# A fused decoder block on one core: the operand sums of the first feed-forward chunk split over several slots, and the chunk loops written out

## The chip, the cores and the metric

The kernel runs on one NeuronCore of a Trainium2 chip. The metric is the device time of one launch in microseconds (us), the median over several runs.

## What is computed

One decoder layer on 256 tokens of width 2048, in float32: a SwiGLU feed-forward (FFN1), a mixer (short gated convolution beside sparse attention), a second SwiGLU (FFN2), and a last RMSNorm.

```python
def rmsnorm(x, g):
    xf = x.astype(jnp.float32)
    y = xf * lax.rsqrt(jnp.mean(xf * xf, axis=-1, keepdims=True) + EPS)
    return (y * g.astype(jnp.float32)).astype(x.dtype)

def swiglu(h, wg, wu, wd):
    return (jax.nn.silu(h @ wg) * (h @ wu)) @ wd

    x = x + 0.5 * swiglu(rmsnorm(x, ffn1_norm[i]), ffn1_wg[i], ffn1_wu[i], ffn1_wd[i])
    x = x + hybrid_mixer(rmsnorm(x, mix_norm[i]), w_in[i], ...)
    x = x + 0.5 * swiglu(rmsnorm(x, ffn2_norm[i]), ffn2_wg[i], ffn2_wu[i], ffn2_wd[i])
return rmsnorm(x, final_norm)
```

Only the gate and up parts of the two feed-forwards matter here: (256 x 2048) times (2048 x 5632), twice.

## The kernel before

**Numbers.** Each float32 product is made from three matmuls. An operand is split into a high part (rounded, on ScalarE) and a low part (the rest, on VectorE), and `hi*hi + hi*lo + lo*hi` is summed in PSUM. The transposed activations are `hT_hi` and `hT_lo` (16 tiles of 128 rows), a weight block is `w_hi` and `w_lo`.

**Slots.** The whole kernel is a row of slots. A slot is one weight block of 2 x 128 rows by 512 columns (512 KB). SyncE loads it into one of four buffers `raw`, and waits for that until VectorE has finished the block that lay there (`lo_ready`). ScalarE makes `w_hi` (L1307), VectorE `w_lo` (L1825), TensorE multiplies it by both token tiles: 12 matmuls of 512 columns (L768 to L770, function `group`). Every engine has its own instruction queue, written in slot order with other work put between slots by hand-made tables (`after`), and the engines meet only in semaphores.

**Pairs (seven products).** Some neighbouring slots (kinds `PAIR`, `PAIR2`) are done by a Strassen-like scheme with 7 block products for 8 (`seven_products`, L786 to L788). It needs sums of the four 128 x 128 activation blocks of a "quad" (two k tiles by two token tiles), called `hs`, and sums of weight blocks, called `wt` (VectorE `weight_sums`, L1887 to L1892, and `wt_low`, L1897; ScalarE L1358). Three quads of a feed-forward have activation sums; quad number 0 belongs to k tiles 2 and 3, numbers 1 and 2 to tiles 4 to 7. `hs` holds four blocks a quad, split again into `hs_hi` (ScalarE, `hs_high`, L1389) and `hs_lo` (VectorE, `hs_low`, L1934). The function `h_sums` makes `hs`: one addition of `hT_hi` and `hT_lo` (L1921), two sums that need only that (L1925, L1926), then a third (L1928) that needs the first, and a fourth (L1930) that needs the third.

**Chunks.** The 5632 columns are 11 chunks of 512, 16 slots each. Chunk 0 has the table `FIRST`, the others `CHUNK` or, for chunks 5, 6 and 10, `CHUNK3`. Quads 1 and 2 are used in every chunk (the pairs of `FIRST` stand in slots 8, 9 and 12, 13), quad 0 in `CHUNK3` alone:

```python
FIRST = [(GATE, 0), (GATE, 1), (UP, 0), (UP, 1), (GATE, 4), (GATE, 5), (UP, 4), (UP, 5),
         (PAIR, 2), (PAIR2, 2), (GATE, 6), (GATE, 7), (PAIR, 3), (PAIR2, 3), (UP, 6), (UP, 7)]
THREE = (5, 6, 10)
LATE = (0,) + THREE
H_QUAD = {1: 0, 2: 1, 3: 2}
```

In chunk 0 of FFN1 the activations are still being brought in. TensorE transposes x four k tiles at a time between slots (L835), ScalarE and VectorE make `hT_hi` (L1330) and `hT_lo` (L1853) of them ("operand n"), ScalarE also squares x for the norm (`sq`, L1343), and VectorE makes the variance (L1866, L1870). What stands behind which slot of chunk 0 of FFN1 on VectorE:

```python
after = {2: [op[1]], 3: [lambda: h_sums(0)], 4: [op[2]], 5: [lambda: hs_low(0)],
         6: [op[3], lambda: variance(RS_FFN1, DM, NDC)],
         7: [lambda: inverse_root(RS_FFN1)]}
```

**From chunk 0 to chunk 1.** Chunk 0 is `LATE`: its products are only gathered in the first slots of chunk 1. ScalarE copies product 1 to `z` when the second pair is done (L1385), VectorE adds it to the gate's bank (L1956, `gate_products`), ScalarE applies silu to the first token tile (a table load, then L1399), makes `w_hi` of slot 1, and applies silu to the second tile. TensorE may begin chunk 1 only after both silus (`silu_done`), since it writes the same banks. `h_sum` shares its memory with `z`.

**Loops.** On TensorE, ScalarE and VectorE chunks 2, 3, 4 and chunks 8, 9 of each feed-forward are turns of a hardware loop (`Fori`), in which waits compare with registers. The other chunks are written out. GpSimd moves the gated product `gu` with DMAs in a loop of its own. Between chunk 5 and 6, and at the end, stand the down projections (`down`).

**In chunk n** VectorE also makes the sums `gs` of chunk n - 1's gated product (`gu_sums`, L2037 to L2042) and the low parts (`gu_operand`: L2050 for `guT_lo`, L2055 for `gs_lo`); `quad_no` says whether the chunk has such sums: it has for chunks 0 to 3 and 6 to 8.

## Time and profile before

| | us |
|---|---|
| median of 3 runs (lowest 1814.9, highest 1815.92) | 1815.18 |
| the profiled execution | 1815.7 |
| its span, from the first to the last instruction | 1813.9 |
| TensorE matmuls busy | 1802.4 |
| VectorE busy | 1534.1 |
| ScalarE busy | 1017.5 |
| GpSimd busy | 247.0 |

The profiled execution took 0.5 us more than the median, and 1.8 us of it lie outside the span. Busy times are of one engine each and overlap. A matmul is listed with a modelled length (0.39 us for 512 columns) that is longer than the time from one start to the next (0.227 us), since matmuls are pipelined: gaps of TensorE are therefore read from start to start. The granted clock of TensorE is 0.999 over the span.

### The profile page before, as it was taken

The numbers are of one execution on the slowest core, as the hardware profiler recorded it, in microseconds if no ns is written. First come the engines' busy times: TensorE is split into PE (matmuls) and PEld (weight loads), VectorE is DVE, ScalarE is ACT, GpSimd is POOL, SyncE is SP. The second block draws the span as 40 slices with busy tenths as digits, with TensorE's granted clock in tenths as the row PEclk, the third lists the DMA queues.
The fourth block names the chain that finished last, engine by engine and source line by source line (L and its number), as shares of the span: only waits on it lengthen the run. The fifth ranks groups of instructions, "written<-read, shape, count | busy, mean of one in ns | idle before, by whom it ended". The sixth has DMA issues, their size and how long they took to land.

```text
span 1813.9 us, 22660 instructions
## 1 busy us (share of the span) xinstructions
PE 1802.4 (99%) x8151; PEld 1485.4 (82%) x8152; DVE 1534.1 (85%) x1821; ACT 1017.5 (56%) x1320; POOL 247.0 (14%) x442
## 2 busy tenths in 40 slices
PE   9999999999999999999999999999999999999998
PEld 6888888888888888888788888888888888888886
DVE  7998898889999987678667867899898889988987
ACT  7555555445555556556577745555555455555554
POOL 2111111001111100000123300111111000221100
PEclk9999999999999999999999999999999999999999
DMA  7777766667676666766543655667766666777764
GB/s 244 220 211 212 217 206 211 206 200 218 211 211 207 215 199 210 209 212 195 150 137 108 209 175 185 215 211 214 213 205 207 215 204 195 216 213 217 246 200 150
DMA packets 199277, 367.13 MB, mean 202 GB/s; under 512 B 19012, under 2 KB 23856, under 8 KB 199056
## 3 DMA queue, kind: packets, MB, share of 16 engines
q1 hardware_dynamic: 185008, 352.37, 63.2%
q0 software_dynamic: 11648, 12.02, 2.2%
q10 hardware_dynamic: 2528, 1.52, 0.3%
q8 instruction: 56, 0.92, 0.2%
q14 instruction: 37, 0.30, 0.1%
...
## 4 chain that ended last, share of the span: by engine, by line
PE 97%; DVE 1%; ACT 1%; DMA 0%; issue 0%; SPq 0%; ACTq 0%; DVEq 0%
PE ps L768 25%; PE ps L770 24%; PE ps L769 24%; PE ps L786 7%; PE ps L787 7%; PE ps L788 7%; PE ps L835 1%; DMA raw<-in_ffn_wu_dram 0%; DVE w_lo L1825 0%; PE ps L1071 0%; PE ps L1098 0%; PE ps L1073 0%; PE ps L1099 0%; PE ps L1201 0%; ACT w_hi L1307 0%
## 5 line engine op out<-in xcount | busy, mean ns | idle before, releaser
L1825 DVE TENSOR_TENSOR w_lo<-raw,w_hi 128x1024 fp32r<-128x1024 f32 x579 | 702.1, 1227 | 132.6 <-ACT w_hi L1307 127.9
L1307 ACT ACTIVATE w_hi<-raw 128x1024 fp32r<-128x1024 f32 x579 | 609.4, 1058 | 357.4 <-PE ps L770 271.5
L768 PE MATMUL ps<-w_hi,hT_hi 128*128 128x512 f32 x1356 | 531.1, 392 | 1.2 <-DVE hT_lo L1853 1.1
L770 PE MATMUL ps<-w_hi,hT_lo 128*128 128x512 f32 x1356 | 528.3, 390 | 0.0
L769 PE MATMUL ps<-w_lo,hT_hi 128*128 128x512 f32 x1356 | 528.0, 389 | 0.0
L709 POOL DMA_DIRECT2D gu_raw<-gu_sq x352 | 187.1, 540 | 1077.3 <-DVE gu_sq L2061 1003.0
L768 PEld LDWEIGHTS ps<-w_hi,hT_hi 128*128 128x128 f32 x1356 | 254.7, 188 | 53.7 <-DVE hT_lo L1853 1.5
L770 PEld LDWEIGHTS ps<-w_hi,hT_lo 128*128 128x128 f32 x1356 | 254.5, 188 | 53.8
L769 PEld LDWEIGHTS ps<-w_lo,hT_hi 128*128 128x128 f32 x1356 | 254.7, 188 | 51.5
L1358 ACT ACTIVATE wt_hi<-wt 128x1024 fp32r<-128x1024 f32 x152 | 160.2, 1054 | 230.2 <-DVE wt L1887 230.2
L768 PE MATMUL ps<-w_hi,guT_hi 128*128 128x512 f32 x496 | 193.1, 389 | 0.0
L770 PE MATMUL ps<-w_hi,guT_lo 128*128 128x512 f32 x496 | 193.0, 389 | 0.0
L769 PE MATMUL ps<-w_lo,guT_hi 128*128 128x512 f32 x496 | 193.0, 389 | 0.0
L1897 DVE TENSOR_TENSOR wt_lo<-wt,wt_hi 128x1024 fp32r<-128x1024 f32 x152 | 185.3, 1219 | 0.0
L770 PEld LDWEIGHTS ps<-w_hi,guT_lo 128*128 128x128 f32 x496 | 93.1, 188 | 19.4
L768 PEld LDWEIGHTS ps<-w_hi,guT_hi 128*128 128x128 f32 x496 | 93.1, 188 | 19.3
L769 PEld LDWEIGHTS ps<-w_lo,guT_hi 128*128 128x128 f32 x496 | 93.1, 188 | 19.2
L1887 DVE TENSOR_TENSOR wt<-raw 128x1024 f32<-128x1024 f32 x76 | 93.0, 1224 | 15.1 <-PE ps L788 10.5
L731 POOL TENSOR_SCALAR prob<-prob,sums,gate 128x128 f32<-128x128 f32 (+1 forms) x64 | 37.2, 590 | 258.8 <-DVE sums L2323 258.8
L786 PE MATMUL ps<-wt_hi,hs_hi 128*128 128x512 f32 x150 | 58.6, 391 | 0.8 <-DVE wt_lo L1897 0.7
L788 PE MATMUL ps<-wt_hi,hs_lo 128*128 128x512 f32 x150 | 58.4, 389 | 0.0
L787 PE MATMUL ps<-wt_lo,hs_hi 128*128 128x512 f32 x150 | 58.4, 389 | 0.0
...
## 6 DMA issues: line engine op xcount, KB each, us to landing
...
```

Source lines behind the costliest of these rows:

```text
L709: pool.dma_start(gu_raw[c_ * SQ:c_ * SQ + SQ, :, a_, :], gu_sq[a_ * SQ:a_ * SQ + SQ, :, c_ * P:c_ * P + P]).then_inc(gu_moved, 16)
L768: mm(o, x_hi, w_hi[:, s, kk, :], start=begin, stop=False, skip_group_check=skip)
L769: mm(o, x_hi, w_lo[:, s, kk, :], start=False, stop=False, skip_group_check=skip)
L770: ins = mm(o, x_lo, w_hi[:, s, kk, :], start=False, stop=last and kk == GK - 1, skip_group_check=skip)
L786: mm(o, x_hi, y_hi, start=start, stop=False, skip_group_check=True)
L787: mm(o, x_hi, y_lo, start=False, stop=False, skip_group_check=True)
L788: return mm(o, x_lo, y_hi, start=False, stop=stop, skip_group_check=True)
L1307: act.activation(w_hi[:, c % SLOTS, :, :], raw[:, c % SLOTS, :, :], ACT.Copy).then_inc(hi_ready, 1)
L1358: act.activation(wt_hi[:, 2 * half:2 * half + 2, :], wt[:, 2 * half:2 * half + 2, :], ACT.Copy).then_inc(t_hi_ready, 1)
L1825: tt(w_lo[:, s, :, :], raw[:, s, :, :], w_hi[:, s, :, :].bitcast(F32), ALU.subtract).then_inc(lo_ready, 1)
L1887: tt(wt[:, T1:T3 + 1, :], w[:, 2, :].unsqueeze(1).to_broadcast([P, 2, CH]), w[:, 0::3, :], ALU.subtract).then_inc(t1_ready, 1)
L1897: tt(wt_lo[:, sl, :], wt[:, sl, :], wt_hi[:, sl, :].bitcast(F32), ALU.subtract).then_inc(t_lo_ready, 1)
```

## The change

Three things are done.

1. The activation sums of chunk 0 are made in pieces, in both feed-forwards. `h_sums(f, late, step)` works on quads 1 and 2 (`late` 0) or on quad 0 (`late` 1), and its step 1 is the third and fourth sum. On VectorE in FFN1 step 0 for two quads stays behind slot 3, step 1 stands behind slot 5, and `hs_low` for two quads behind slot 6. In FFN2 both steps stay behind slot 2. Quad 0 follows behind slot 14 in both, its `hs_low` behind slot 8 of chunk 1. On ScalarE `hs_high` for two quads moves in FFN1 from behind slot 4 to behind slot 5, ahead of the squares of x; for quad 0 it stands behind slot 15. TensorE waits for two quads before the first pair of chunk 0, and for quad 0 before the first pair of chunk 5 (`THREE[0]`).
2. The subtraction that makes `gs_lo` is taken out of `gu_operand` into `gs_low`, which stands behind slot 14 in `CHUNK3` chunks and behind the same slot as before in the others.
3. The hardware loops over chunks on TensorE, ScalarE and VectorE are replaced by written-out chunks. GpSimd's loop stays.

```diff
@@ TensorE @@
                     if p == chunk_pairs(0)[0]:
-                        pe.wait_ge(hs_lo_ready, f + 1)
+                        pe.wait_ge(hs_lo_ready, 2 * f + 1)
...
                     for p, (kind, q) in enumerate(chunk_table(n)):
+                        if n == THREE[0] and p == at_[0]:
+                            pe.wait_ge(hs_lo_ready, 2 * f + 2)
...
-                chunk(1)
-                with pe.Fori(0, QUADS[0] - 1) as i:
-                    chunk(2, i)
-                for n in range(QUADS[0] + 1, PARTN[0]):
+                for n in range(1, PARTN[0]):
                     chunk(n)
                 down(0)
-                chunk(PART0[1])
-                chunk(PART0[1] + 1)
-                with pe.Fori(0, QUADS[1] - 1) as i:
-                    chunk(PART0[1] + 2, i)
-                for n in range(PART0[1] + QUADS[1] + 1, NFC):
+                for n in range(PART0[1], NFC):
                     chunk(n)
                 down(1)
@@ ScalarE @@
-            def hs_high(f):
-                act.wait_ge(hs_ready, f + 1)
-                act.activation(hs_hi[:, :, :, :], hs[:, :, :, :], ACT.Copy).then_inc(hs_hi_ready, 1)
+            def hs_high(f, late):
+
+                sl = slice(0, 1) if late else slice(1, 3)
+                act.wait_ge(hs_ready, 2 * f + late + 1)
+                act.activation(hs_hi[:, sl, :, :], hs[:, sl, :, :], ACT.Copy).then_inc(hs_hi_ready, 1)
...
-                    after = {1: [sq[0]], 2: [op[1]], 3: [sq[1]], 4: [op[2], lambda: hs_high(0)],
-                             5: [sq[2]], 6: [op[3], sq[3]], 7: [lambda: root(RS_FFN1)], 10: [vectors]}
+                    after = {1: [sq[0]], 2: [op[1]], 3: [sq[1]], 4: [op[2]],
+                             5: [lambda: hs_high(0, 0), sq[2]], 6: [op[3], sq[3]], 7: [lambda: root(RS_FFN1)], 10: [vectors], 15: [lambda: hs_high(0, 1)]}
                 else:
-                    after = {2: [lambda: x_square(RS_FFN2, NDC - 1, resid(R_ATT, NDC - 1))], 3: [lambda: hs_high(1)],
-                             5: [lambda: x_operand(2, NDC - 1)], 6: [lambda: root(RS_FFN2)]}
+                    after = {2: [lambda: x_square(RS_FFN2, NDC - 1, resid(R_ATT, NDC - 1))], 3: [lambda: hs_high(1, 0)],
+                             5: [lambda: x_operand(2, NDC - 1)], 6: [lambda: root(RS_FFN2)], 15: [lambda: hs_high(1, 1)]}
@@ VectorE @@
+            def h_sums(f, late, step):
+
+
+                sl = slice(0, 1) if late else slice(1, 3)
+                no, k0, quads = 2 * f + late + 1, 2 if late else 4, 1 if late else 2
+                h = h_sum[:, sl, :].rearrange("p q (r t) -> p q r t", r=2)
                 block_ = lambda t, kk: h[:, :, kk, t * P:t * P + P]
...
+                o = lambda n: hs[:, sl, n - 1, :]
+                if step == 0:
+                    for b in range(2):
+                        dve.wait_ge(free[4 + b], operand_use(2 if f else 0, b, 1) + 1)
+                    pick = lambda buf: buf[:, k0:k0 + 2 * quads, :].rearrange("p (q r) t -> p q r t", q=quads)
+                    tt(h, pick(hT_hi).bitcast(F32), pick(hT_lo).bitcast(F32), ALU.add).then_inc(hs_full, 1)
+                    dve.wait_ge(hs_full, no)
+                    tt(o(1), block_(1, 0), block_(1, 1), ALU.add).then_inc(hs1_ready, 1)
+                    tt(o(3), block_(1, 0), block_(0, 0), ALU.subtract)
+                else:
+                    dve.wait_ge(hs1_ready, no)
+                    tt(o(2), o(1), block_(0, 0), ALU.subtract).then_inc(hs2_ready, 1)
+                    dve.wait_ge(hs2_ready, no)
+                    tt(o(4), block_(0, 1), o(2), ALU.subtract).then_inc(hs_ready, 1)
...
-                if quad is not None:
-                    dve.wait_ge(gs_hi_ready, count(quad + 1, i, 1))
-                    low, buf, high = gs_parts(n, i)
-                    ins = tt(low, buf, high.bitcast(F32), ALU.subtract)
-                ins.then_inc(gu_lo, 1)
+                if quad is None:
+                    ins.then_inc(gu_lo, 1)
+
+            def gs_low(n, quad, i=None):
+
+                if quad is not None:
+                    dve.wait_ge(gs_hi_ready, count(quad + 1, i, 1))
+                    low, buf, high = gs_parts(n, i)
+                    tt(low, buf, high.bitcast(F32), ALU.subtract).then_inc(gu_lo, 1)
...
-                    after = {2: [op[1]], 3: [lambda: h_sums(0)], 4: [op[2]], 5: [lambda: hs_low(0)],
-                             6: [op[3], lambda: variance(RS_FFN1, DM, NDC)],
+                    after = {2: [op[1]], 3: [lambda: h_sums(0, 0, 0)], 4: [op[2]], 5: [lambda: h_sums(0, 0, 1)],
+                             6: [op[3], lambda: hs_low(0, 0), lambda: variance(RS_FFN1, DM, NDC)],
                              7: [lambda: inverse_root(RS_FFN1)]}
...
+                after[14] = [lambda: h_sums(f, 1, 0), lambda: h_sums(f, 1, 1)]
...
+                            if n == 1 and p == 8:
+                                hs_low(f, 1)
...
+                            if p == (14 if n in THREE else gu_at + 1):
+                                gs_low(n - 1, quad_no(f, n - 1), i)
```

(ScalarE's and VectorE's loops are replaced as TensorE's.) The line numbers in the changed kernel differ from those before: on VectorE the `h_sum` addition is L1916, the four sums L1918, L1919, L1922, L1924, `hs_lo` L1930, `w_lo` L1815 and operands L1843; on ScalarE `w_hi` is L1302, `hs_hi` L1386, operands L1325 and squares L1338.

VectorE in FFN1, chunk 0, from slot 3 to slot 6, before. A bracket names the semaphores that an instruction waits for.

```order
L1825 TENSOR_TENSOR w_lo<-raw,w_hi 128x1024 [waits hi_ready]
L1921 TENSOR_TENSOR h_sum<-hT_hi,hT_lo 128x1536 [waits bank_free5,bank_free4]
L1925 TENSOR_TENSOR hs<-h_sum 128x3x128 [waits hs_full]
L1926 TENSOR_TENSOR hs<-h_sum 128x3x128
L1928 TENSOR_TENSOR hs<-hs,h_sum 128x3x128 [waits hs1_ready]
L1930 TENSOR_TENSOR hs<-h_sum,hs 128x3x128 [waits hs2_ready]
L1825 TENSOR_TENSOR w_lo<-raw,w_hi 128x1024 [waits hi_ready]
```

The same place now; the four rows of operand 2 stand between:

```order
L1815 TENSOR_TENSOR w_lo<-raw,w_hi 128x1024 [waits hi_ready]
L1916 TENSOR_TENSOR h_sum<-hT_hi,hT_lo 128x1024 [waits bank_free5,bank_free4]
L1918 TENSOR_TENSOR hs<-h_sum 128x2x128 [waits hs_full]
L1919 TENSOR_TENSOR hs<-h_sum 128x2x128
L1815 TENSOR_TENSOR w_lo<-raw,w_hi 128x1024 [waits hi_ready]
L1843 SCALAR_TENSOR_TENSOR hT_lo<-ps,vecs,hT_hi 128x256 [waits operand_hi]
L1843 SCALAR_TENSOR_TENSOR hT_lo<-ps,vecs,hT_hi 128x256
L1843 SCALAR_TENSOR_TENSOR hT_lo<-ps,vecs,hT_hi 128x256 [waits operand_hi]
L1843 SCALAR_TENSOR_TENSOR hT_lo<-ps,vecs,hT_hi 128x256
L1815 TENSOR_TENSOR w_lo<-raw,w_hi 128x1024 [waits hi_ready]
L1922 TENSOR_TENSOR hs<-hs,h_sum 128x2x128 [waits hs1_ready]
L1924 TENSOR_TENSOR hs<-h_sum,hs 128x2x128 [waits hs2_ready]
```

The third and fourth sum, which `hs_high` waits for, moved behind the `w_lo` of slot 5, and all sums are two quads wide, not three.

ScalarE in the same stretch, from operand 2's last instructions to the `w_hi` of slot 6, before:

```order
L1330 ACTIVATE hT_hi<-ps,vecs 128x256
L1389 ACTIVATE hs_hi<-hs 128x1536 [waits hs_ready]
L1307 ACTIVATE w_hi<-raw 128x1024 [waits group_done,landed1]
L1343 ACTIVATE junk,ssq<-x 128x512 [waits x_landed2]
L1343 ACTIVATE junk,ssq<-x 128x512 [waits act_step]
L1307 ACTIVATE w_hi<-raw 128x1024 [waits act_step,group_done,landed2]
```

Now:

```order
L1325 ACTIVATE hT_hi<-ps,vecs 128x256
L1302 ACTIVATE w_hi<-raw 128x1024 [waits group_done,landed1]
L1386 ACTIVATE hs_hi<-hs 128x1024 [waits hs_ready]
L1338 ACTIVATE junk,ssq<-x 128x512 [waits x_landed2]
L1338 ACTIVATE junk,ssq<-x 128x512 [waits act_step]
L1302 ACTIVATE w_hi<-raw 128x1024 [waits act_step,group_done,landed2]
```

`hs_hi` and the `w_hi` of slot 5 changed places; the squares and the `w_hi` of slot 6 stay behind both.

VectorE from the end of the second pair of chunk 0 to the gate's addition (the same in both feed-forwards), now; before, the five rows from `h_sum` to the last `hs` were not there:

```order
L1887 TENSOR_TENSOR wt_lo<-wt,wt_hi 128x1024 [waits t_hi_ready]
L1815 TENSOR_TENSOR w_lo<-raw,w_hi 128x1024 [waits hi_ready]
L1916 TENSOR_TENSOR h_sum<-hT_hi,hT_lo 128x512 [waits bank_free5,bank_free4]
L1918 TENSOR_TENSOR hs<-h_sum 128x128 [waits hs_full]
L1919 TENSOR_TENSOR hs<-h_sum 128x128
L1922 TENSOR_TENSOR hs<-hs,h_sum 128x128 [waits hs1_ready]
L1924 TENSOR_TENSOR hs<-h_sum,hs 128x128 [waits hs2_ready]
L1815 TENSOR_TENSOR w_lo<-raw,w_hi 128x1024 [waits hi_ready] x2
L1952 TENSOR_TENSOR ps<-ps,z 128x512 [waits prod1_copied]
```

Five instructions stand new between slot 14's `w_lo` and the two `w_lo` of slot 15 and of chunk 1's slot 0.

## Rows read from the trace of the kernel before

**Rows 1.** First part of the page: busy time, share, instructions

```profile
PE 1802.4 (99%) x8151; PEld 1485.4 (82%) x8152; DVE 1534.1 (85%) x1821; ACT 1017.5 (56%) x1320; POOL 247.0 (14%) x442
```

**Rows 2.** Timeline, PE, chunk 0 of FFN1: start us, us, instruction [idle before <-releaser]

```profile
20.77 0.39 PE L770 MATMUL ps<-w_hi,hT_lo 128*128 128x512 f32 x1
22.25 0.50 PE L768 MATMUL ps<-w_hi,hT_hi 128*128 128x512 f32 x1 [1.09 <-DVE hT_lo L1853]
...
36.61 0.50 PE L786 MATMUL ps<-wt_hi,hs_hi 128*128 128x512 f32 x1 [0.73 <-DVE wt_lo L1897]
...
37.67 0.50 PE L786 MATMUL ps<-wt_hi,hs_hi 128*128 128x512 f32 x1
```

**Rows 3.** Windows, chunk 2 of FFN1: us, busy (x) PE PEld DVE ACT POOL, clock

```profile
99.68:143.20 43.52, 43.52 (x193) 36.04 (x192) 38.98 (x46) 22.81 (x25) 8.50 (x16) 1.00 0.75 224
```

**Rows 4.** Timeline, DVE, slots 3 to 5 of chunk 0 of FFN1

```profile
16.40 1.75 DVE L1921 TENSOR_TENSOR h_sum<-hT_hi,hT_lo 128x1536 f32<-128x1536 f32 x1
...
18.66 0.55 DVE L1926 TENSOR_TENSOR hs<-h_sum 128x384 f32<-128x384 f32 x1
19.13 0.55 DVE L1928 TENSOR_TENSOR hs<-hs,h_sum 128x384 f32<-128x384 f32 x1
19.72 0.56 DVE L1930 TENSOR_TENSOR hs<-h_sum,hs 128x384 f32<-128x384 f32 x1
20.20 1.22 DVE L1825 TENSOR_TENSOR w_lo<-raw,w_hi 128x1024 fp32r<-128x1024 f32 x1
21.33 1.65 DVE L1853 SCALAR_TENSOR_TENSOR hT_lo<-ps,vecs,hT_hi 128x256 fp32r<-128x256 f32 x4
```

**Rows 5.** Timeline, ACT, slots 4 to 10 of chunk 0 of FFN1

```profile
18.03 1.57 ACT L1330 ACTIVATE hT_hi<-ps,vecs 128x256 fp32r<-128x256 f32 x4 [0.50 <-PE ps L835]
...
21.70 1.04 ACT L1307 ACTIVATE w_hi<-raw 128x1024 fp32r<-128x1024 f32 x1
22.65 0.61 ACT L1343 ACTIVATE junk<-x 128x512 bf16<-128x512 f32 x1
...
24.28 1.06 ACT L1307 ACTIVATE w_hi<-raw 128x1024 fp32r<-128x1024 f32 x1 [0.17 <-ACT junk L1343]
...
28.90 1.06 ACT L1307 ACTIVATE w_hi<-raw 128x1024 fp32r<-128x1024 f32 x1 [0.17 <-ACT junk L1343]
...
37.38 0.23 ACT L1299 ACTIVATE vecs<-ps 128x104 f32<-128x104 f32 x1
```

**Rows 6.** Timeline, DVE, slots 7 and 8 of chunk 0 of FFN1

```profile
30.00 1.30 DVE L1825 TENSOR_TENSOR w_lo<-raw,w_hi 128x1024 fp32r<-128x1024 f32 x1 [0.56 <-ACT w_hi L1307]
...
31.41 1.23 DVE L1825 TENSOR_TENSOR w_lo<-raw,w_hi 128x1024 fp32r<-128x1024 f32 x1
32.56 1.41 DVE L1887 TENSOR_TENSOR wt<-raw 128x1024 f32<-128x1024 f32 x1
```

**Rows 7.** Timeline, DVE, ACT and PE where FFN1's chunk 1 begins

```profile
47.26 3.49 DVE L1825 TENSOR_TENSOR w_lo<-raw,w_hi 128x1024 fp32r<-128x1024 f32 x3
51.55 0.70 DVE L1956 TENSOR_TENSOR ps<-ps,z 128x512 f32<-128x512 f32 x1 [0.80 <-ACT z L1385]
...
55.16 0.68 ACT L1399 ACTIVATE gu<-ps,rs 128x512 f32<-128x512 f32 x1
...
56.16 0.39 PE L768 MATMUL ps<-w_hi,hT_hi 128*128 128x512 f32 x1
```

**Rows 8.** Timeline, DVE, the same place in FFN2

```profile
1146.66 3.61 DVE L1825 TENSOR_TENSOR w_lo<-raw,w_hi 128x1024 fp32r<-128x1024 f32 x3
1151.92 0.70 DVE L1956 TENSOR_TENSOR ps<-ps,z 128x512 f32<-128x512 f32 x1 [1.65 <-ACT z L1385]
```

**Rows 9.** Timeline, DVE, 128-wide sums in chunk 1 of FFN1

```profile
84.80 0.29 DVE L2037 TENSOR_TENSOR gs<-gu_raw 128x128 f32<-128x128 f32 x1
...
85.20 0.29 DVE L2040 TENSOR_TENSOR gs<-gs,gu_raw 128x128 f32<-128x128 f32 x1
85.53 0.29 DVE L2042 TENSOR_TENSOR gs<-gu_raw,gs 128x128 f32<-128x128 f32 x1
```

More of the change, by code:

```diff
@@ L1491, in down @@
                                 x_operand(1, 0)
-                chunk(1)
-                with act.Fori(0, QUADS[0] - 1) as i:
-                    chunk(2, i)
-                for n in range(QUADS[0] + 1, PARTN[0]):
+                for n in range(1, PARTN[0]):
                     chunk(n)
                 down(0)
-                chunk(PART0[1])
-                chunk(PART0[1] + 1)
-                with act.Fori(0, QUADS[1] - 1) as i:
-                    chunk(PART0[1] + 2, i)
-                for n in range(PART0[1] + QUADS[1] + 1, NFC):
+                for n in range(PART0[1], NFC):
                     chunk(n)
@@ L1935, in hs_low @@
+            def hs_low(f, late):
+                sl = slice(0, 1) if late else slice(1, 3)
+                dve.wait_ge(hs_hi_ready, 2 * f + late + 1)
+                tt(hs_lo[:, sl, :, :], hs[:, sl, :, :], hs_hi[:, sl, :, :].bitcast(F32),
                    ALU.subtract).then_inc(hs_lo_ready, 1)
@@ L2161, in down @@
                                 final_gains((23, 25, 39).index(g))
-                chunk(1)
-                with dve.Fori(0, QUADS[0] - 1) as i:
-                    chunk(2, i)
-                for n in range(QUADS[0] + 1, PARTN[0]):
+                for n in range(1, PARTN[0]):
                     chunk(n)
                 down(0)
-                chunk(PART0[1])
-                chunk(PART0[1] + 1)
-                with dve.Fori(0, QUADS[1] - 1) as i:
-                    chunk(PART0[1] + 2, i)
-                for n in range(PART0[1] + QUADS[1] + 1, NFC):
+                for n in range(PART0[1], NFC):
                     chunk(n)
```

22 lines of the change are left out of this document (3 added, 19 removed).

## The prediction

> **What bounds the kernel now.** I read the page first: TensorE's matmuls are busy 1802.4 us of a span of 1813.9 [rows 1], so only what shortens or lengthens TensorE's waits can change the time. Then I looked for every place where two matmuls start further apart than usual. In a chunk the usual distance is 43.52 us / 192 = 0.227 us [rows 3]. In the timeline of TensorE three waits stand in chunk 0 of FFN1 [rows 2]: 20.77 to 22.25, which is 1.48 - 0.23 = **1.25 us**; before 36.61, where the profile lists 0.73 idle and the listed length of a matmul (0.39) hides another 0.16, so **0.9 us**; and at 37.67, three matmuls (0.68) and a start-up of 0.11 behind 36.61, so **0.27 us**. Together 2.4 us. From 38 us to the end of FFN1, and in FFN2, I found none.
>
> The timelines of VectorE and ScalarE say what the three wait for. The first waits for operand 2: VectorE made the sums for slots 8 and up (16.40 to 20.20) ahead of slot 4's `w_lo` and of `hT_lo` [rows 4]. The second waits for the first `wt_lo` of the pair. VectorE works without a pause from 30.00, and at 30.00 it had waited for ScalarE's `w_hi` of slot 7, which began at 28.90 [rows 5, 6]. The third waits for ScalarE's `vecs` at 37.38, behind the `w_hi` of slot 10 [rows 5]; it follows the second.
>
> **Part 1a, chunk 0 of FFN1.** Distances to the next start, from rows: a 1024-wide operation 1.14 (20.20 to 21.33), a 384-wide one 0.47, 0.59 where the next needs its result, a 128-wide one 0.20 and 0.33 [rows 4, 9]; so 256 wide lies between, 0.34 and 0.45. An addition of 1024 (1.22 long) with a dependent behind it takes 1.26.
>
> - VectorE: `h_sum` 16.40, sums 17.66 and 18.00, `w_lo` of slot 4 at 18.34 (before: 20.20), operand 2 at 19.48, its first half (two of four) ready at 20.4. TensorE can begin slot 4 at 21.00, right behind slot 3. **The first wait goes: 1.25 us gained.**
> - Operand 2 ends at 21.05 (1.57, 21.33 to 22.90 less overlap), `w_lo` of slot 5 follows until 22.19, third sum 22.19, fourth 22.64, `hs_ready` at 23.06.
> - ScalarE: operand 2 from 18.03 as before, since TensorE's transposes don't move; `w_hi` of slot 5 at 19.5 to 20.55 (before: 21.70). Then `hs_hi` stands in its queue and **waits 2.5 us**, until 23.09. Behind it are queued the squares and the `w_hi` of slot 6. A 1024-wide `hs_hi` takes 0.95 like a `w_hi` (21.70 to 22.65), the squares 1.63 (22.65 to 24.28) [rows 5]: `w_hi` of slot 6 at 25.67, before 24.28, **1.4 us later**. Operand 3 (1.44, no longer waiting for its transposes) and squares (1.67): `w_hi` of slot 7 at 29.74, before 28.90, 0.85 later.
> - VectorE waits for slot 6's `w_hi` until 26.76, then `w_lo`, operand 3 (1.57), `hs_lo` of 1024 (1.14) until 30.6, two small operations of the variance (0.2 each, as the 128-wide) until 31.0: `w_lo` of slot 7 at 31.0, before 30.00. `w_lo` of slot 8 follows at 32.35 and the weight sums at 33.5, before 32.56. The first weight sum took 1.41 there and a 1024-wide one takes 1.22; GpSimd's casts lay beside it and come 2 us earlier now, so 0.2 comes back. The `wt_lo` that TensorE waits for is **0.7 us later** than before.
> - TensorE: slot 6 now waits about 0.5 us, slot 7 (its `w_lo` ready at 32.2) about 1.4, the pair 0.8, `vecs` 0.27 as before. That is 3.1 us where 2.4 stood. **Net +0.7 us.** Bounds: below, all waits gone, -2.4; above, ScalarE's 2.5 us of waiting handed on whole, +2.5. I take +0.7, since each step of the chain has its row.
>
> The loads of slots 8 to 12 are issued when `w_lo` of four slots before is done, and shift with it by -1.9 to +1.0 us; in the chain above every `w_hi` has its data by then.
>
> **Part 1b, quad 0 behind slot 14.** New on VectorE: 0.73 for a 512-wide addition with a dependent, then 0.20 + 0.20 + 0.33 + 0.20 [rows 9] = **1.66 us**, and on ScalarE a 512-wide `hs_hi` (0.5), each ahead of something that is due. The three `w_lo` from 47.26 (slots 14, 15, and slot 0 of chunk 1) are 1.14 apart [rows 7]. With T = 48.4, the end of the first: the fourth sum starts at T + 1.46 and ends 0.29 on, `hs_hi` starts at T + 1.78, slot 0's `w_hi` at T + 2.3 (1.06 long), its `w_lo` at T + 3.4, the gate's addition at T + 4.5 = 52.9. Before it stood at 51.55, and VectorE had idled 0.80: **1.36 us later**. The chain behind it (addition, table load, silu, `w_hi`, silu) keeps its length, and its end at 55.16 + 0.68 = 55.84 is what TensorE waits for at chunk 1, which began at 56.16 [rows 7]. Less 0.05 for the semaphore, the slack was 0.27: **+1.1 us**. In FFN2 VectorE idled 1.65, not 0.80, before the same addition [rows 8]: with T = 1147.80 the addition comes at 1152.32, before 1151.92, 0.40 later, less 0.27: **+0.1 us**. Bounds for each: 0 if the work fits the idle time after all; 1.66 + 0.5 - 0.27 = 1.9 if all of it stands in the chain.
>
> The low part of quad 0 (512 wide, 0.61) behind slot 8 of chunk 1 costs nothing: VectorE idles 43.52 - 38.98 = 4.5 us in a chunk like it [rows 3]. If that cover were gone it would cost 0.6 a feed-forward. TensorE's new wait for quad 0 in chunk 5 is met some 150 us earlier. In FFN2 sums and `hs_lo` of two quads for three only relieve VectorE, where TensorE did not wait; 0.
>
> **Part 2, `gs_low`.** In `CHUNK3` chunks (5, 6, 10) it would run for chunk 4 or 9, which have no such sums (`quad_no` is None), or not at all; elsewhere it stands where it stood. Nothing moves; 0.
>
> **Part 3, loops written out.** Ten turns of a loop go on each of three engines. The row of chunk 2, from its first matmul to chunk 3's, with the loop's turn in it, has 43.52 us for 192 distances, 0.2267 each, none longer [rows 3]: the turn is hidden behind the matmuls in flight. On the other two engines it is short beside the idle time. 0, and the bounds are 0 and what the rival below gives.
> The Trainium skill (Advanced Engine Details and Errata, Sequencer and Instruction Queues, Control Flow Timing) gives about 51 ns for a branch and about 108 ns for a compare-and-branch; ten turns at 159 ns would be a gain of 1.6 us, and the sum would be +0.3 us. The trace doesn't agree: no distance at the turn is longer.
>
> **Sum.** +0.7 + 1.1 + 0.1 = **+1.9 us**. Against the profiled execution, 1815.7 + 1.9 = 1817.6 us (span 1815.8); it stood 0.5 above the median, and against the median 1815.18 it is **1817.1 us**. About 0.2% (3.6 us) is what a measurement of this kernel can tell from no change, so this forecast counts as no change.
>
> **The rivals.**
> - *The first wait goes and doesn't come back* (0.15). If ScalarE's wait for `hs_ready` is absorbed and slot 7's `w_lo` follows VectorE's shortened work, the pair starts about 1.2 us earlier: with part 1b as above 1815.2, with 1b hidden too 1814.0. For it: VectorE has 1.9 us less ahead of slot 4. Against: `hs_hi` sits ahead of the `w_hi` of slot 6 in a strict queue, and VectorE can't do slot 6 without that.
> - *Loop turns cost TensorE something* (0.04). Starting a turn would add its branches to TensorE's stream; 1.6 us come back over ten turns: 1815.5. Against: the even distances. It is also the price of the rule cited above.
> - *VectorE has no room left in chunk 1* (0.05, the slower side). The gate's addition comes 1.4 us late and `hs_lo` of quad 0 adds 0.6. If the weight sums of chunk 1's pairs then come after TensorE needs them, all late work is exposed in both feed-forwards: 0.7 + 2 x (1.9 + 0.6) = 5.7, 1820.9 us. It decides where VectorE's lead over TensorE at chunk 1's first pair is under about 1 us; for it speaks that VectorE is busy 38.98 of 43.52 us in a chunk, against it that it idles in every chunk and catches up.
> - *The change doesn't do what it says* is true of part 2, and priced 0.
>
> **How the numbers follow.** Forecast 0.74, the rivals 0.15, 0.04, 0.05, something unseen 0.02. All PE waits of chunk 0 together are 2.4 us, less than 0.2%, so faster by over 0.2% is left with 0.02; slower by over 0.2% gets the third rival and a part of the unseen, 0.06; within 0.2% 0.92. The range reaches from the first rival's middle, 1814.4, to 1818.6, where 1a and FFN2's 1b each come out 0.8 worse.
>
> **What would show it.** In the profile after: slot 4 starts at 21.00 with no wait before; `hs_hi` waits about 2.5 us for `hs`; the `w_lo` of slot 7 starts at 31.0; waits of 0.5 and 1.4 us before TensorE's slots 6 and 7; the pair's first `wt` product at 37.3; the gate's addition about 52.9 + 0.7 and a wait of about 1.1 us where chunk 1 begins, 0.1 in FFN2; no change in the distances at chunks 2 to 5. The prediction is wrong if slot 7's `w_lo` stands before 30.5, if chunk 1 begins without a wait, or if a chunk that was a loop's turn takes other than 43.52 us.

## The result, and the profile after

| | before, us | after, us |
|---|---|---|
| median of 17 runs each | 1815.92 | 1819.54 |
| lowest | 1814.9 | 1818.27 |
| the profiled execution | 1815.7 | 1819.37 |
| its span | 1813.9 | 1817.6 |
| TensorE matmuls busy | 1802.4 | 1805.3 |
| VectorE busy | 1534.1 | 1534.6 |

The ratio of the times is 1.0019, with a 95% interval of 1.0012 to 1.0026: the changed kernel is 3.6 us slower, just inside the 0.2% that was taken as the limit. One of the 17 runs of the changed kernel took 2983 us, with a mean granted clock of 0.568, and moves the median by less than 0.1 us; no later run repeated it. The forecast was 1817.1 us (1814.4 to 1818.6): the sign is right, but the time lies 0.9 us above the range.

First the page of the changed kernel, part 1, to be held against [rows 1], and then the view of waits, TensorE (us in total, times, longest).

```profile
PE 1805.3 (99%) x8151; PEld 1486.7 (82%) x8152; DVE 1534.6 (84%) x1833; ACT 1017.4 (56%) x1322; POOL 246.0 (14%) x442
...
PE ps L768 <- DVE w_lo L1815: 1.5, 2, 1.1
...
PE ps L768 <- ACT gu L1396: 0.7, 1, 0.7
...
PE ps L786 <- DVE wt_lo L1887: 0.6, 1, 0.6
```

The work is the same: VectorE has 12 instructions more and 0.5 us more. "PE busy" has grown by 2.9 us with the same 8151 matmuls; 2.0 us of that lie ahead of the first product, as the start of the timeline will show. The wait for `hT_lo` L1853 [rows 2] is gone, two new ones stand there: on `w_lo`, and on `gu`, the silu. Of the 1.5 us on `w_lo`, 1.1 stand at slot 7 and 0.4 in the mixer.

Timeline of TensorE in the changed kernel: slot 4 (22.64), slots 6 and 7, the first pair, chunk 1 in FFN1 and in FFN2.

```profile
22.41 0.39 PE L770 MATMUL ps<-w_hi,hT_lo 128*128 128x512 f32 x1
22.64 0.39 PE L768 MATMUL ps<-w_hi,hT_hi 128*128 128x512 f32 x1
...
28.74 0.39 PE L770 MATMUL ps<-w_hi,hT_lo 128*128 128x512 f32 x1
29.24 0.50 PE L768 MATMUL ps<-w_hi,hT_hi 128*128 128x512 f32 x1
...
31.87 0.39 PE L770 MATMUL ps<-w_hi,hT_lo 128*128 128x512 f32 x1
33.35 0.50 PE L768 MATMUL ps<-w_hi,hT_hi 128*128 128x512 f32 x1 [1.09 <-DVE w_lo L1815]
...
37.47 0.40 PE L788 MATMUL ps<-w_hi,hT_lo 128*128 128x512 f32 x1
38.45 0.50 PE L786 MATMUL ps<-wt_hi,hs_hi 128*128 128x512 f32 x1 [0.59 <-DVE wt_lo L1887]
...
57.79 0.39 PE L770 MATMUL ps<-w_hi,hT_lo 128*128 128x512 f32 x1
58.92 0.50 PE L768 MATMUL ps<-w_hi,hT_hi 128*128 128x512 f32 x1 [0.74 <-ACT gu L1396]
...
1159.72 0.39 PE L770 MATMUL ps<-w_hi,hT_lo 128*128 128x512 f32 x1
1160.07 0.50 PE L768 MATMUL ps<-w_hi,hT_hi 128*128 128x512 f32 x1
```

Start to start, less the usual 0.227: no wait at slot 4; 0.50 - 0.23 = 0.27 at slot 6; 1.48 - 0.23 = 1.25 at slot 7; 0.98 - 0.23 = 0.75 at the pair; 1.13 - 0.23 = 0.90 at chunk 1; 0.35 - 0.23 = 0.12 in FFN2. Each wait is followed by 0.11 us more, since the second matmul behind it starts 0.34 us after the first, not 0.23. The pair and chunk 1 come 1.84 and 2.76 us later than in [rows 2, 7].

Timeline of VectorE, then that of ScalarE, in the same chunk.

```profile
18.96 1.22 DVE L1815 TENSOR_TENSOR w_lo<-raw,w_hi 128x1024 fp32r<-128x1024 f32 x1
...
23.81 0.43 DVE L1924 TENSOR_TENSOR hs<-h_sum,hs 128x256 f32<-128x256 f32 x1
...
27.96 1.23 DVE L1815 TENSOR_TENSOR w_lo<-raw,w_hi 128x1024 fp32r<-128x1024 f32 x1 [3.73 <-ACT w_hi L1302]
...
32.08 1.22 DVE L1815 TENSOR_TENSOR w_lo<-raw,w_hi 128x1024 fp32r<-128x1024 f32 x1
...
51.50 0.29 DVE L1924 TENSOR_TENSOR hs<-h_sum,hs 128x128 f32<-128x128 f32 x1
51.71 1.22 DVE L1815 TENSOR_TENSOR w_lo<-raw,w_hi 128x1024 fp32r<-128x1024 f32 x1
53.44 1.23 DVE L1815 TENSOR_TENSOR w_lo<-raw,w_hi 128x1024 fp32r<-128x1024 f32 x1 [0.51 <-ACT w_hi L1302]
54.59 0.69 DVE L1952 TENSOR_TENSOR ps<-ps,z 128x512 f32<-128x512 f32 x1
```

```profile
21.11 1.07 ACT L1302 ACTIVATE w_hi<-raw 128x1024 fp32r<-128x1024 f32 x1
24.27 1.06 ACT L1386 ACTIVATE hs_hi<-hs 128x1024 fp32r<-128x1024 f32 x1 [2.09 <-DVE hs L1924]
...
26.87 1.06 ACT L1302 ACTIVATE w_hi<-raw 128x1024 fp32r<-128x1024 f32 x1 [0.17 <-ACT junk L1338]
...
30.93 1.06 ACT L1302 ACTIVATE w_hi<-raw 128x1024 fp32r<-128x1024 f32 x1 [0.17 <-ACT junk L1338]
```

`hs_hi` stands in ScalarE's queue for 2.09 us; behind it `w_hi` of slot 6 (26.87) is late, VectorE idles 3.73 us for it, and then `w_lo` of slot 7 (32.08) is late behind operand 3 and `hs_lo`. VectorE was relieved of 1.9 us and lost all of it, and more, to that idle time. Behind slot 14 the sums of quad 0 end at 51.79, `w_hi` and `w_lo` of chunk 1's slot 0 follow, and the gate's addition stands at 54.59.

**The part nobody forecast** is in the first ten microseconds. Timeline of TensorE, before, and then the changed kernel; both programs are the same there.

```profile
5.52 0.66 PE L862 MATMUL ps<-consts,x 128*128 128x128 f32 x4
6.21 0.63 PE L835 MATMUL ps<-consts,x 128*128 128x128 f32 x4
6.67 1.46 PE L893 MATMUL ps<-junk 128*128 128x512 bf16 x6
8.19 0.50 PE L877 MATMUL ps<-w_hi,hT_hi 128*128 128x512 f32 x1
```

```profile
5.23 1.12 PE L862 MATMUL ps<-consts,x 128*128 128x128 f32 x4
6.14 1.06 PE L835 MATMUL ps<-consts,x 128*128 128x128 f32 x4
6.99 2.77 PE L893 MATMUL ps<-junk 128*128 128x512 bf16 x6
9.82 0.50 PE L877 MATMUL ps<-w_hi,hT_hi 128*128 128x512 f32 x1
```

Junk matmuls are products that nobody reads, issued to occupy TensorE; `WARM` in the kernel says how many, seven at the very start and six ahead of the first product. The same six take 1.46 us there and 2.77 here: the clock stands at its 1.2 GHz level until 9.69 us after the changed kernel's start, and came to 2.4 GHz at 4.81 us in the kernel before (times of the first clock record in each trace). The first product starts 1.63 us later. The mean granted clock doesn't tell the two apart: it is 0.999 in both profiles. The Trainium skill (TensorE: Matmul & The Clock Gate, What's actually happening) says that the array starts at the lower level, that its activity releases it, and that the number of slow matmuls at a kernel's start differs from run to run; the traces agree, with 4.81 against 9.69, and with 9.69, 4.60 and 3.84 in three profiles of the changed kernel (after, e4, e16).

So of 3.7 us between the two profiles up to 1.6 might be a different execution and not the change. Matched matmul by matmul, the difference is 1.63 at the first product, 1.85 at the pair, 2.89 behind the start of chunk 1, 2.73 in the mixer at 808 us, 3.55 at 841 us and 3.71 at the end. The 0.8 us in the mixer, where the change edits nothing, stand in no term of the prediction either.

### The profile page after: what moved, and what is told of

Read it like the earlier page. It is cut to its first block, busy times and chain, and to the rows that moved or that the text cites. A ratio compares the mean times of both kernels' runs of the same rounds, so it can differ in the third digit from the quotient of the medians.

```text
span 1817.6 us, 21938 instructions
## 1 busy us (share of the span) xinstructions
PE 1805.3 (99%) x8151; PEld 1486.7 (82%) x8152; DVE 1534.6 (84%) x1833; ACT 1017.4 (56%) x1322; POOL 246.0 (14%) x442
## 4 chain that ended last, share of the span: by engine, by line
PE 96%; DVE 2%; ACT 1%; DMA 0%; issue 0%; ACTq 0%; SPq 0%; DVEq 0%
PE ps L768 24%; PE ps L770 24%; PE ps L769 24%; PE ps L786 7%; PE ps L788 7%; PE ps L787 7%; PE ps L835 2%; DVE w_lo L1815 1%; ACT w_hi L1302 0%; PE ps L1066 0%; PE ps L1093 0%; PE ps L1068 0%; PE ps L1094 0%; DMA raw<-in_cmp_v_w_dram 0%; PE ps L1196 0%
## 5 line engine op out<-in xcount | busy, mean ns | idle before, releaser
L1815 DVE TENSOR_TENSOR w_lo<-raw,w_hi 128x1024 fp32r<-128x1024 f32 x579 | 702.3, 1227 | 141.5 <-ACT w_hi L1302 136.8
L1302 ACT ACTIVATE w_hi<-raw 128x1024 fp32r<-128x1024 f32 x579 | 609.3, 1057 | 356.5 <-PE ps L770 276.8
```

The costliest lines, as they stand in the source:

```text
L1302: act.activation(w_hi[:, c % SLOTS, :, :], raw[:, c % SLOTS, :, :], ACT.Copy).then_inc(hi_ready, 1)
L1815: tt(w_lo[:, s, :, :], raw[:, s, :, :], w_hi[:, s, :, :].bitcast(F32), ALU.subtract).then_inc(lo_ready, 1)
```

## The experiments

The expectations name theories by letters. A: the change costs its own waits, 1.9 us. B: the clock comes early or late by chance of an execution, and a late one costs 1.6 us. C: the written-out loops move the clock or something in the mixer. D: what the changed kernel costs beyond its waits comes from executions with a late clock; D1 says that a late clock costs both kernels the same, D2 that it costs the changed one more, since the kernel before has a wait at slot 4 that takes up some of it. Every kernel ran 11 times, in batches of four kernels on one chip, each batch with 33 runs of the kernel before; differences between batches are therefore less sure than those within one. "Clock" is the time of the first record of the 2.4 GHz level in the profiled execution; the other executions of a kernel don't show theirs.

| kernel | median us | ratio to before | span us | clock us |
|---|---|---|---|---|
| e1_before | 1816.59 | 1.0001 [0.9992, 1.001] | 1814.0 | 4.54 |
| e2_unroll | 1817.12 | 1.0004 [0.9995, 1.0013] | 1815.6 | 9.50 |
| e3_split | 1818.82 | 1.0012 [1.0003, 1.0021] | 1817.3 | 8.97 |
| e4_after | 1819.4 | 1.0016 [1.0006, 1.0025] | 1816.3 | 4.60 |
| e5_late_moved | 1817.82 | 1.0009 [1.0, 1.0018] | 1815.5 | 8.56 |
| e6_hs_order | 1817.65 | 1.001 [1.0001, 1.0019] | 1815.0 | 4.13 |
| e7_both | 1814.91 | 0.9996 [0.9987, 1.0005] | 1813.1 | 4.26 |
| e8_warm | 1815.46 | 0.9997 [0.9988, 1.0006] | 1813.6 | 6.82 |
| e9_after_warm | 1817.67 | 1.001 [1.0001, 1.0019] | 1815.5 | 4.01 |
| e10_unroll_warm | 1816.03 | 1.0 [0.9991, 1.0009] | 1813.2 | 4.23 |
| e11_best | 1813.94 | 0.9987 [0.9978, 0.9996] | 1812.1 | 5.21 |
| e12_before_warm | 1815.48 | 0.9998 [0.9989, 1.0007] | 1813.5 | 3.96 |
| e13_before_cold | 1816.61 | 1.0002 [0.9993, 1.0011] | 1815.0 | 10.18 |
| e14_after_cold | 1819.12 | 1.0015 [1.0006, 1.0024] | 1818.2 | 10.79 |
| e15_before | 1816.2 | 0.9999 [0.999, 1.0008] | 1813.5 | 5.66 |
| e16_after | 1818.87 | 1.0015 [1.0006, 1.0024] | 1816.1 | 3.84 |

The kernel before, 33 runs in each batch (e1 to e4, e5 to e8, e9 to e12, e13 to e16), had medians of 1816.42, 1816.14, 1816.40 and 1815.95.

### The parts of the change (e1 to e4)

e1_before and e4_after are the two kernels again. e2_unroll is the kernel before with the loops alone written out, on TensorE, ScalarE and VectorE:

```diff
-                chunk(1)
-                with pe.Fori(0, QUADS[0] - 1) as i:
-                    chunk(2, i)
-                for n in range(QUADS[0] + 1, PARTN[0]):
+                for n in range(1, PARTN[0]):
```

e3_split is the changed kernel with those loops put back (the same lines, the other way round).

> The kernel before, unchanged, as its own comparison. Theory A (the extra time is the split sums' own waits, +1.9 us): ratio 1.000, and the profile may open TensorE's clock at either time, 4.8 or 9.7 us. Theory B (the clock opens late by chance of one execution): runs of this kernel spread by about 1.2 us and more, and another profile of it shows the late opening in some executions. Theory C (the written-out loops move the opening of the clock or something in the mixer): the clock opens at 4.8 us again and the mixer has the same waits as in the profile before.

> The kernel before with the chunk loops written out and nothing else. Theory A: 0 us against before, waits of 1.25, 0.9 and 0.27 us in chunk 0 as before, no wait at chunk 1. Theory C: +1.5 us or more, the clock opening late or new waits in the mixer.

> The changed kernel with the hardware loops kept: the split sums alone. Theory A: +1.9 us against before, of it 0.7 in chunk 0 and about 1 at chunk 1 of FFN1. Theory C: +1.9 as well, but the changed kernel then stands another 1.7 above it. If all +3.6 us are here, the sums cost more than their waits in the trace.

> The changed kernel again on the same chip. +3.6 us against before as measured; theory B: another profile of it opens the clock at some other time than 9.7 us while the time stays about the same.

e4 showed an early clock this time, so that e1 and e4 can be compared directly. Timeline of TensorE in e1_before (slot 4 and the first pair), and then in e4_after (slots 6 and 7, the first pair, chunk 1).

```profile
21.54 0.50 PE L768 MATMUL ps<-w_hi,hT_hi 128*128 128x512 f32 x1 [0.56 <-DVE hT_lo L1853]
...
35.90 0.50 PE L786 MATMUL ps<-wt_hi,hs_hi 128*128 128x512 f32 x1 [0.74 <-DVE wt_lo L1897]
```

```profile
27.49 0.50 PE L768 MATMUL ps<-w_hi,hT_hi 128*128 128x512 f32 x1 [0.23 <-DVE w_lo L1815]
...
31.60 0.50 PE L768 MATMUL ps<-w_hi,hT_hi 128*128 128x512 f32 x1 [1.09 <-DVE w_lo L1815]
...
36.70 0.50 PE L786 MATMUL ps<-wt_hi,hs_hi 128*128 128x512 f32 x1 [0.58 <-DVE wt_lo L1887]
...
57.17 0.50 PE L768 MATMUL ps<-w_hi,hT_hi 128*128 128x512 f32 x1 [0.74 <-ACT gu L1396]
```

The pair stands at 36.70 for 35.90, **+0.80**. Matmul by matmul the difference then grows by 0.91 at chunk 1 of FFN1 and by 0.13 at chunk 1 of FFN2, each with another 0.11 behind it, and by 0.36 in the mixer between them; the spans differ by 2.3. (The wait at slot 4 that the change takes away was 0.72 in e1, for 1.25 in the first profile.) On VectorE `w_lo` of slot 7 moved by 1.06 and the gate's addition by 1.98.

Unrolling: the difference of e2 against e1 in the trace (1.92 at the first product, 1.64 at the pair, 1.65 at the end) comes from the first ten microseconds, with a clock at 9.50 instead of 4.54; no distance at a chunk's turn differs. A late clock isn't the loops' doing, as theory C had it: e3 has the loops and a late one (8.97), e4 has none and an early one (4.60). The rule quoted from the Trainium skill in the prediction (Advanced Engine Details and Errata, Control Flow Timing) would have made e2 1.6 us faster by the prediction's estimate; neither trace nor median (1.0004) shows a gain. Its median is 0.7 us above the batch's before and e3's 0.6 below e4's, both within the intervals, though both on the slower side. Part of the 0.7 lies outside the span: the time of an execution less its span is 2.08 to 2.22 us in all runs of e2, and 1.75 to 1.89 in those of the kernel before and of every kernel with the split sums. Why, no run shows.

### Taking the two mechanisms away (e5, e6, e7)

e5_late_moved takes quad 0 out of the way of chunk 1's first silu. VectorE's late sums stand behind slot 9 of chunk 1, ScalarE's `hs_high` behind its slot 11, `hs_low` behind slot 9 of chunk 2:

```diff
-                after[14] = [lambda: h_sums(f, 1, 0), lambda: h_sums(f, 1, 1)]
...
-                            if n == 1 and p == 8:
+                            if n == 1 and p == 9:
+                                dve.wait_ge(gu_moved, 16 * QB * QB * (NFC * f + 1))
+                                h_sums(f, 1, 0)
+                                h_sums(f, 1, 1)
+                            if n == 2 and p == 9:
```

e6_hs_order moves ScalarE's first `hs_high` behind other ready work:

```diff
-                             5: [lambda: hs_high(0, 0), sq[2]], 6: [op[3], sq[3]], 7: [lambda: root(RS_FFN1)], 10: [vectors], 15: [lambda: hs_high(0, 1)]}
+                             5: [sq[2]], 6: [lambda: hs_high(0, 0), op[3], sq[3]], 7: [lambda: root(RS_FFN1)], 10: [vectors], 15: [lambda: hs_high(0, 1)]}
```

e7_both has both, and `vectors` behind slot 9 instead of 10.

> The changed kernel with quad 0's sums moved from behind slot 14 of chunk 0 to behind slot 9 of chunk 1, where VectorE idles 2 us. Theory A (the sums hold up the gate's addition): the waits at chunk 1 of 0.9 us in FFN1 and 0.12 in FFN2 vanish, the time falls 1.0 us against the changed kernel, to about +2.2 against before. Rival (the waits there come from something else, or the work is as dear in its new place): no fall, or a new wait at chunk 1's second pair.

> The changed kernel with ScalarE's hs_high moved from behind slot 5, ahead of the squares, to behind slot 6. Theory A (ScalarE's 2.1 us wait for the sums delays the w_hi of slots 6 and 7): the waits before TensorE's slots 6 and 7 (0.3 and 1.25) vanish, the one in the pair shrinks from 0.8 to about 0.3, the w_lo of slot 7 comes near 28.3 where the clock opens early; the time falls 2.0 us against the changed kernel. Rival (VectorE's own work is what delays slot 7): falls less than 0.7.

> Both moves together, and ScalarE's vecs copy behind slot 9, not 10. Theory A: only the pair's first wait of about 0.3 us is left in chunk 0 and none at chunk 1, so some 2 us less waiting than the kernel before and 3.3 less than the changed one: about 1.5 to 2 us faster than before.

In e6 `hs_hi` starts at once (timeline of ScalarE in e6_hs_order), for the price of two squares done first:

```profile
23.03 1.06 ACT L1386 ACTIVATE hs_hi<-hs 128x1024 fp32r<-128x1024 f32 x1
```

The wait before slot 6 is gone and the one before slot 7 is 0.14 us, for 1.25; but the pair, which was expected to wait 0.3, still waits 0.75, and chunk 1's wait grew to 1.07: 1.3 us are left of the gain at the end of the trace against e4, where 2.0 were expected. In e5 the waits at chunk 1 of both feed-forwards are gone and the four of chunk 0 stand as they were; its median is 1.7 us above its batch's kernel before, where 2.2 were expected. In e7 only the pair's wait (0.8) is left of those named. View of waits, TensorE, e7_both:

```profile
...
PE ps L768 <- DVE w_lo L1817: 0.8, 2, 0.4
PE ps L786 <- DVE wt_lo L1889: 0.6, 1, 0.6
```

(The two on `w_lo` stand in the mixer.) Its span is 3.2 us below e4's, and its median 4.5 below that of e4, which is of another batch. Against the kernel before its median is 1.2 us lower (1814.91 for 1816.14), where 1.5 to 2 were expected, and the interval [0.9987, 1.0005] doesn't part the two. What the traces show is that the waits at slots 6 and 7 and at chunk 1 go with the instruction that was said to make each of them.

### The clock at the start (e8 to e16)

Here the first number of `WARM` changes. e8_warm and e12_before_warm are the same kernel, e9 is the changed kernel with that line, e10 is e2 with it, and e11_best is e7 with it:

```diff
-WARM = [7, 6]
+WARM = [9, 6]
```

The two more fill idle time before `vec_rows` lands (0.33 to 1.15 us in the eleven profiles with seven). In e8 and e11 they use all of it, and the matmul on `vec_rows` starts at 5.28 and 5.27, where it started at 4.68 to 5.51 with seven.

> The kernel before with nine instead of seven junk matmuls at the start, which fill the idle time of about 1 us until the first transposes. Theory B (the clock opens at 4.5 or at 9 to 9.7 us by chance of an execution, and a late opening costs 1.6 us): the late openings go, the spread of the runs shrinks from 2.6 us to about 1.5 and the median falls 0.5 to 1 us. Rival (the opening doesn't hang on the idle time): no change in spread or median; the two more junk matmuls cost nothing or 0.1 us.

> The changed kernel with nine junk matmuls at the start. Theory D (what the changed kernel costs beyond its own waits of 1.9 us comes from executions in which the clock opens late): the spread shrinks from 3.4 us to about 1.5, and it stands 1.9 to 2.2 us above e12_before_warm. Rival (the excess is a cost of the written-out loops or of something the profile doesn't show): it stands 3.3 us above e12_before_warm.

> The kernel before with written-out loops and nine junk matmuls. Theory A and D: within 0.3 us of e12_before_warm. Rival (written-out loops cost something outside the waits): 0.7 us or more above it, as e2_unroll stood above before.

> Both moves of e7_both and nine junk matmuls. Theory A and D: 1.5 to 2 us below e12_before_warm and 2.3 to 2.7 us below before, with a spread of about 1.5 us; clear of noise against before.

> The same kernel as e8_warm on the chip of these runs, for comparison: 0.5 to 0.8 us below before, spread about 1.5 us, the clock opening between 4.2 and 7 us.

With nine, the lowest and the highest of 11 runs are 1.1 to 1.5 us apart in the five sets (e8 to e12), where seven gave 1.6 to 3.4 in nine sets of 11 (e1 to e7, e15, e16). The profiles have the clock at 3.96 to 6.82, none at 8.5 or more; with seven, 4 of 11 profiles have it at 8.5 or more, so five early ones alone would prove little, and the narrower times are the better evidence. The medians of e8 and e12 are 0.7 and 0.9 us below those of their batches, about what was expected, but within the intervals. Between kernels that both have nine, **the change costs 1817.67 - 1815.48 = 2.2 us** (e9 against e12), and 1.99 in the two traces: -1.28 at slot 4, +2.01 by slot 7, so +0.73 there, and 1.93 after FFN2's chunk 1. The unrolling (e10 against e12) costs 0.55 us in the medians, where less than 0.3 was expected, and gains 0.25 in the traces. As in e2, about 0.34 of it lies outside the span (2.10 to 2.20 us in all 11 runs, for 1.77 to 1.86). A small cost of the loops in this form is therefore not excluded; what lies outside the span is not found in the changed kernel (1.8). Timeline of TensorE, e11_best, from 3 us on (the first line has six of the nine): the junk matmuls run on to 5.22, and the next six are at full clock:

```profile
2.45 2.77 PE L893 MATMUL ps<-junk 128*128 128x512 bf16 x6
5.27 0.23 PE L858 MATMUL ps<-consts,vec_rows 16*128 16x16 f32 x1
...
6.44 1.46 PE L893 MATMUL ps<-junk 128*128 128x512 bf16 x6
7.96 0.50 PE L877 MATMUL ps<-w_hi,hT_hi 128*128 128x512 f32 x1
```

Still open was why the first comparison gave 3.6. e13_before_cold and e14_after_cold take the clock's early opening away from both kernels, and e15_before and e16_after repeat the two:

```diff
-WARM = [7, 6]
+WARM = [1, 6]
```

> The kernel before with one junk matmul in the first burst, not seven, so that the clock opens late in every execution. Theory D: the time is that of the slow end of before, 1817.3 us or more, about 0.9 above its median, and no execution is as fast as 1815.5. If it is as fast as before, the junk matmuls don't decide the opening.

> The changed kernel in the same way. Theory D1 (a late opening costs both kernels about the same, 1.6 to 1.8 us in the traces, and the changed one merely met it more often): 2.0 to 2.3 us above e13_before_cold, as with nine junk matmuls. Theory D2 (a late opening costs the changed kernel more, since the kernel before has a wait of 1.25 us at slot 4 that takes up some of it): 2.8 us or more above e13_before_cold.

> The kernel before once more, 11 more runs and another opening of the clock: 1816.4 us, between 1814.9 and 1817.5; D1 wants late openings in fewer executions than for the changed kernel.

> The changed kernel once more. D1 and D2: about 3 us above before again, more than with nine junk matmuls. If it is 2.0 to 2.3 us above, the larger differences so far were the luck of few runs.

Timeline of TensorE, e13_before_cold (slot 4 and the pair) and then e14_after_cold: both late.

```profile
6.97 2.77 PE L893 MATMUL ps<-junk 128*128 128x512 bf16 x6
...
22.54 0.39 PE L770 MATMUL ps<-w_hi,hT_lo 128*128 128x512 f32 x1
22.98 0.50 PE L768 MATMUL ps<-w_hi,hT_hi 128*128 128x512 f32 x1
...
37.57 0.50 PE L786 MATMUL ps<-wt_hi,hs_hi 128*128 128x512 f32 x1 [0.96 <-DVE wt_lo L1897]
```

```profile
6.79 2.77 PE L893 MATMUL ps<-junk 128*128 128x512 bf16 x6
...
38.79 0.50 PE L786 MATMUL ps<-wt_hi,hs_hi 128*128 128x512 f32 x1 [0.55 <-DVE wt_lo L1887]
...
59.62 0.50 PE L768 MATMUL ps<-w_hi,hT_hi 128*128 128x512 f32 x1 [1.12 <-ACT gu L1396]
```

With the clock late in both, the change costs 1819.12 - 1816.61 = **2.5 us**; the traces have 1.22 at the pair and 1.27 more at chunk 1, about 0.4 dearer each than with an early clock. (At their ends they are 3.2 apart, but e14's profiled execution was the slowest of its 11.) D1 had said 2.0 to 2.3 and D2 2.8 or more, so the medians decide for neither. The traces show what D2 supposed. In the kernel before, a late clock (e13 against e12) puts TensorE 2.0 us behind ahead of slot 4 and 0.94 behind it, since the wait there shrinks from 1.27 us to 22.98 - 22.54 - 0.23 = 0.21; at the pair it is 1.2. In the changed kernel (e14 against e9), which has no wait at slot 4, it is 2.3 up to there and 1.7 at the pair.

One expectation failed: the kernel before with one junk matmul, and so a late clock in every execution, was to stand at 1817.3 or more, and stands at 1816.61, only 0.66 us above its batch (lowest 1815.63). That is not the price of a late clock, though, since the batch with seven junk matmuls can itself have both kinds of start. Between one junk matmul and nine lie 1816.61 - 1815.48 = 1.1 us for the kernel before (e13, e12) and 1819.12 - 1817.67 = 1.5 us for the changed one (e14, e9), each across two batches. The repeats, clocks at 5.66 and 3.84, gave 1818.87 - 1816.2 = 2.7 us, and 2.63 at the end of the traces.

Another part shows in the mixer, which the change doesn't touch. Timeline of TensorE, index for index the same matmul, before, and then e1_before:

```profile
837.73 0.39 PE L770 MATMUL ps<-w_hi,hT_lo 128*128 128x512 f32 x1
838.05 0.50 PE L768 MATMUL ps<-w_hi,hT_hi 128*128 128x512 f32 x1
```

```profile
837.38 0.39 PE L770 MATMUL ps<-w_hi,hT_lo 128*128 128x512 f32 x1
838.11 0.50 PE L768 MATMUL ps<-w_hi,hT_hi 128*128 128x512 f32 x1 [0.34 <-DVE w_lo L1825]
```

It starts 0.32 us behind its neighbour there and 0.73 here, a wait of 0.09 and of 0.50. In the eight profiles without the split sums this wait is 0.00 to 0.19 in six and 0.50 in two (e1, e2); in the ten profiles with them it is 0.39 to 0.54 in nine and 0.04 in one (e9). A second place, at 821 us, varies from none to 0.62. Over the mixer the changed kernel loses 0.82 us in the first pair of profiles, 0.36 in e4 and e1, 0.58 in e16 and e15, 0.57 in e14 and e13, and 0.15 in e9 and e12. So the wait varies from execution to execution, but it is there in nine of ten profiles with the split sums and in two of eight without: the change seems to bring it on. That, and by which chain, no run shows. The pair e9 and e12, whose sum came nearest to the forecast, is the one in which it was missing.

The profile that the forecast was made from was no odd one: all three profiles of the kernel before have an early clock (4.81, 4.54, 5.66), and two of the three next to no wait in the mixer.

## Why the prediction was wrong, step by step

| step of the prediction | forecast | measured |
|---|---|---|
| wait at slot 4 | gone | gone |
| ScalarE's wait for `hs_ready` | 2.5 | 2.09 (after), 2.20 (e4) |
| waits before slots 6 and 7, pair | 0.5, 1.4, 0.8 | 0.27, 1.25, 0.75 (after); 0.39, 1.25, 0.75 (e4) |
| `w_lo` of slot 7 | +1.0 | +1.06 (e4 against e1) |
| part 1a, net | +0.7 | +0.80 (e4, e1), +0.68 (e9, e12), +0.71 (e16, e15) |
| the gate's addition | 0.7 + 1.36 = 2.06 later | 1.98 later (e4, e1) |
| part 1b, FFN1 and FFN2 | +1.1, +0.1 | +0.91 and +0.13, each with 0.11 behind it |
| the mixer | no term | +0.15 to +0.82 in five pairs of profiles |
| unrolling, `gs_low` | 0, 0 | no changed distance in the traces; medians of the unrolling +0.55 to +0.70 |
| sum | +1.9 | +2.0 in the traces of e9 and e12, +2.2 in their times |

**The mechanism held** to some tenths: the wait goes at slot 4 and comes back at 6 and 7, since `hs_hi` stands ahead of `w_hi` in ScalarE's queue, and quad 0 delays the first silu of chunk 1. The third wait, on `vecs`, stayed at 0.27 as forecast. The rival *the first wait goes and doesn't come back* is refuted by 1.25 us before slot 7, *loop turns cost TensorE something* by e2 and e10, which gained nothing, and *VectorE has no room left in chunk 1* by even distances after chunk 1's start.

**The step that failed is the Sum**: the base of 1815.18 was too low, and the term +1.9 was too small, with nothing in it for the start or for the mixer. The measured median stands 2.4 us above the point and 0.9 above the range.
- *The base.* "Against the median 1815.18" took three runs as the level and corrected the profiled execution by 0.5. Over 17 runs the kernel before has 1815.92, and over 33 runs each 1815.95 to 1816.42. That is 0.7 of the 2.4 us. The profiled execution itself, at 1815.7, was the better base.
- *The difference.* In the first comparison it was 3.6 for a forecast of 1.9; in later batches 3.0 (e4) and 2.9 (e16 against 33 runs), 2.7 (e16 against e15), 2.5 with late clocks, and 2.2 with nine junk matmuls. That is the other 1.7 us.
- *Missing, the start-up.* Each wait costs 0.11 us more than its idle time. The prediction counted that once, before the `vecs` wait. The change takes one wait away and makes four new ones, so three times 0.11 = 0.3 us were left out.
- *Missing, the mixer.* The prediction speaks of waits in the two feed-forwards alone; the mixer had 0.15 to 0.82 us of the difference.
- *Missing, the start.* A clock that comes at 4 or at 9 us makes 1.6 us at the first product. A rival "the same kernel, the late clock" would have stretched the range upwards by some 1.1 to 1.5 us (one junk matmul against nine), and 1819.5 would have been in it.

Small slips in its working change little. The waits 0.5, 1.4, 0.8 and 0.27 add up to 2.97, not 3.1, which leaves a net of +0.55 for part 1a; with the start-up of 0.11 (two new waits for one) that is 0.66, close to what was measured, so +0.7 came out right partly by luck. The middle of the first rival's 1815.2 and 1814.0 is 1814.6, and 1817.1 with 0.8 twice is 1818.7; neither would have taken in 1819.54. GpSimd's casts were to come 2 us earlier; the `cmask_b` casts began 0.4 us earlier (29.77 for 30.16), and the weight sum did take 1.22 for 1.41.

What stays open is how the 1.4 us between 3.6 and 2.2 divide. A late clock costs the changed kernel more in the traces (1.22 + 1.27 in place of 0.80 + 0.91), but the medians with one junk matmul give only 0.3 of it (2.5 for 2.2). Whether the changed kernel also gets a late clock more often is not shown. Of three profiles each, one of the changed kernel's was late and none of before's. Its three medians with seven junk matmuls (1819.54, 1819.40, 1818.87) lie near its time with one junk matmul (1819.12), while those of the kernel before (1815.92 to 1816.59) lie between its times with nine and with one (1815.48, 1816.61); that fits, but proves nothing. Nor is it shown how much was the luck of 17 runs.

**Better than both kernels** is e11_best: the change with the late sums in chunk 1, `hs_high` behind the `w_hi` of slot 6, `vectors` behind slot 9 and nine junk matmuls: 1813.94 us, ratio 0.9987 with an interval of 0.9978 to 0.9996, 2.5 us less than before and 1.5 less than the kernel before with nine (e12). Its interval lies below 1, though the size is under the 0.2% of the text above.
